# Two-layer hybrid encoder: the slots of four gates, of two placings, of one key head and of one low part

## The chip, the cores and the metric

The kernel runs on one core of a Trainium2 chip. The metric is the device time of one execution in microseconds (us). The engines are TensorE (PE: matrix products and transposes), VectorE (DVE), ScalarE (ACT), GpSimd (POOL) and SyncE (SP, here only a DMA queue). They run their own instruction streams and meet at semaphores.

## What is computed

Two layers (`DEPTH` 2) on 512 tokens of width 1024, float32. Each layer norms its input, projects it into 32 column heads of 128, runs four heads of differential attention and four heads of a gated linear recurrence in both directions, projects the eight head outputs back, and adds a convolutional gated feed-forward part of width 2816. Cut to what matters:

```
h = rms_norm(x, mix_norm_g[l])
proj = h @ w_in[l]
da_q, da_k, da_v, hg_q, hg_zf, hg_zb, hg_i, hg_g = split_cols(proj, IN_SIZES)
y_a = diff_attention(da_q, da_k, da_v, cos, sin, ...)   # q, k normed per half head, then rotated
y_b = hgrn2_bidirectional(hg_q, hg_zf, hg_zb, hg_i, hg_g, lower_bounds[l, 0], lower_bounds[l, 1], hg_out_g[l])
x = x + jnp.concatenate([y_a, y_b], axis=-1) @ w_out[l]
x = x + conv_glu_ffn(rms_norm(x, ffn_norm_g[l]), w_up[l], conv_w[l], conv_b[l], w_down[l])

def gates(z, lb):            # per head and direction
    log_f = log_sigmoid(z) + log1p(lb * exp(minimum(-z, 30)))
    key = (1 - lb) * sigmoid(-z)
```

In layer 0 the lower bounds are zero, so a gate there is only its sigmoids.

## The kernel before

**Products in parts.** Every weight and every large input is split into a high part (`wH`, `hH`, `yH`) and a low part (`wL`, `hL`, `yL`), and a product is three matmuls: high by high, low by high, high by low (lines 582 to 584). A *unit* is one weight tile of 128 by 1024. It is loaded into `raw` by SyncE, ScalarE copies its high part (`high_now`, line 914), and GpSimd subtracts to get the low part (`split`, line 512); in the eight slots `SPLITS` (7 to 14) VectorE does that (line 1431). A unit of the input projection is 24 matmuls over 512 tokens.

**Slots.** The mixer of a layer is written as 40 slots, `for s in range(SLOTS)`, on every engine. In slot s TensorE projects unit s in two halves, and the other engines do what hangs on the unit before it. The table `ORDER` says which head part unit s is: `dq`, `dk`, `dv` of attention, `hq`, `zf`, `zb`, `hi`, `hg` of the recurrence. Units 32 to 39 are the output projection. VectorE evicts unit s - 1 in slot s (`evict`, line 1348).

**What else a slot holds.** Each engine works through its stream in order, so the place of a call in the slot's body sets who waits for whom.

- Items 0 to 23 (`item_of`, from slot 7 on), twelve for each pair of recurrent heads. Items 0 to 7 are the levels of the intra-block scores: TensorE multiplies (line 672), VectorE grows the queries `QQ` by the forget products (line 1463), GpSimd grows the keys `KK` (line 545), ScalarE copies the keys crosswise to `kx` (line 1014). Levels 0 to 5 are gathered by masks in a small tile `quarters()`. Levels 6 and 7 stay in their banks 2 and 3. `assemble` on ScalarE places these three results in the score tile `A`: the gathered diagonal quarters (line 1026) and level 6 in the slot of item 6, level 7 in the slot of item 7 (line 1033). Items 8 and 9 (`TURN_F`, `TURN_B`) turn the keys to `KTOK` (line 686), item 10 (`CARRY`) multiplies them with the values (line 701) for VectorE's states `ST` (lines 1489 and 1491), and item 11 gathers everything.
- Steps 0 to 15 of attention (`step_of`, from slot 17 on), one query tile of one head each: scores (line 729), row maximum (line 1500), exponentials (line 1055), one slot later `combine` on VectorE (lines 1506 to 1511), the turn of `W` on TensorE (line 738), the copy `wT` on ScalarE (line 1047), and the values (line 747).
- Statistics (`STATS`: slot to head), the mean square of a head. ScalarE squares it (lines 971 and 972), VectorE forms the low part of the square (`square_low`, line 1383), TensorE multiplies by a mean matrix (`stat`, lines 632 and 633) at the end of the slot, and one slot later ScalarE makes the reciprocal root (`fin`, lines 948 and 951) and VectorE applies it: `rope` with rotary tables for `dk` and `dq` (lines 1360 to 1366), `norm` for outputs.
- `forget(i)`, four VectorE instructions (lines 1408 to 1411) that finish gate i in layer 1, by the table `FORGET`. In layer 0 VectorE instead prepares the rotary tables in the slots `ROTARY`, and the lower bounds in slot 16 (`bounds`).
- In slots 31 to 34 `FINISH` lists the output heads whose high part (`high_out`, ScalarE) and low part (`low_out`, VectorE, line 1397) are formed.

In slot 13 ScalarE also loads an activation table (line 938), and in layer 0 makes the sine and cosine (lines 1144 and 1145).

## Time and profile before

| | |
|---|---|
| median of 3 runs | 1372.3 us (1371.53 to 1372.79) |
| the profiled execution | 1371.9 us, of which the span of its instructions is 1370.1 |
| TensorE busy | 1341.0 us (98%) |
| VectorE busy | 914.3 us (67%) |
| ScalarE busy | 642.2 us (47%) |
| GpSimd busy | 661.0 us (48%) |
| TensorE busy from 0 to 345 us (layer 0, mixer) | 330.94 us |
| TensorE busy from 345 to 665 us (layer 0, feed-forward) | 320.00 us |
| TensorE busy from 665 to 1025 us (layer 1, mixer) | 348.03 us |
| TensorE busy from 1025 to 1370 us (layer 1, feed-forward) | 341.99 us |

Times of the trace count from the start of the span. A row of a timeline reads: start, duration, engine, line, operation, output from inputs, and how many; in brackets the engine's idle time ahead of it and whose result ended it. A duration of a row with "x4" covers the four. TensorE's matmuls overlap by some tenths of a microsecond, since a row runs to the modelled end of its results. Slot 13 of layer 0 begins at 88.0, slot 14 at 94.9; in layer 1 slot 13 begins at 768.5 and slot 14 at 775.3.

### The profile page before, as it was taken

The numbers are of one execution on the slowest core, as the hardware profiler recorded it, in microseconds if no ns is written. First come the engines' busy times: TensorE is split into PE (matmuls) and PEld (weight loads), VectorE is DVE, ScalarE is ACT, GpSimd is POOL, SyncE is SP. The second block draws the span as 40 slices with busy tenths as digits, with TensorE's granted clock in tenths as the row PEclk, the third lists the DMA queues.
The fourth block names the chain that finished last, engine by engine and source line by source line (L and its number), as shares of the span: only waits on it lengthen the run. The fifth ranks groups of instructions, "written<-read, shape, count | busy, mean of one in ns | idle before, by whom it ended". The sixth has DMA issues, their size and how long they took to land.

```text
span 1370.1 us, 20822 instructions
## 1 busy us (share of the span) xinstructions
PE 1341.0 (98%) x7970; PEld 1086.1 (79%) x7970; DVE 914.3 (67%) x1058; ACT 642.2 (47%) x948; POOL 661.0 (48%) x475
## 2 busy tenths in 40 slices
PE   9999999999999999999999999999999999999999
PEld 6777777877888888888877777778778888888887
DVE  7777898555888888600358789975658888885001
ACT  7453677574444444321443636666644444443121
POOL 2553565246444444444565536752474444444443
PEclk9999999999999999999999999999999999999999
DMA  5322122122332332333322222121233333333333
GB/s 186 94 78 85 51 71 74 46 63 92 100 100 92 96 105 92 93 106 96 92 93 94 78 70 71 55 70 46 78 92 94 105 94 93 102 98 92 95 104 108
DMA packets 37140, 121.43 MB, mean 89 GB/s; under 512 B 5056, under 2 KB 5440, under 8 KB 37056
## 3 DMA queue, kind: packets, MB, share of 16 engines
q1 hardware_dynamic: 36768, 119.75, 28.3%
q8 instruction: 58, 0.95, 0.3%
q10 hardware_dynamic: 288, 0.52, 0.1%
q14 instruction: 26, 0.21, 0.0%
HBM read 113.96 MB, written 2.10 MB: 85 GB/s over the span
## 4 chain that ended last, share of the span: by engine, by line
PE 77%; DVE 10%; ACT 5%; issue 4%; POOL 3%; DMA 0%; ACTq 0%; DVEq 0%; POOLq 0%
PE bank L582 23%; PE bank L584 23%; PE bank L583 23%; DVE QQ L1463 2%; PE bank L729 2%; POOL wL L518 1%; PE bank L747 1%; PE bank L672 1%; DVE hL L420 1%; POOL KK L545 1%; ACT wH L914 1%; POOL rstd L432 1%; PE bank L738 1%; PE bank L701 1%; ACT L938 1%
## 5 line engine op out<-in xcount | busy, mean ns | idle before, releaser
L518 POOL TENSOR_TENSOR wL<-raw,wH 128x1024 fp32r<-128x1024 f32 x142 | 344.2, 2424 | 403.3 <-ACT wH L914 293.1
L582 PE MATMUL bank<-hH,wH 128*128 128x512 f32 x1216 | 484.9, 399 | 2.1 <-DVE hL L420 2.0
L584 PE MATMUL bank<-hL,wH 128*128 128x512 f32 x1216 | 475.7, 391 | 0.0
L583 PE MATMUL bank<-hH,wL 128*128 128x512 f32 x1216 | 475.0, 391 | 0.0
L582 PEld LDWEIGHTS bank<-hH,wH 128*128 128x128 f32 x1216 | 229.2, 188 | 65.4 <-issue 14.5
L512 POOL TENSOR_TENSOR wL<-raw,wH 128x256 fp32r<-128x256 f32 x204 | 184.8, 935 | 197.4 <-ACT wH L914 197.4
L584 PEld LDWEIGHTS bank<-hL,wH 128*128 128x128 f32 x1216 | 229.0, 188 | 49.0
L583 PEld LDWEIGHTS bank<-hH,wL 128*128 128x128 f32 x1216 | 229.3, 189 | 45.4 <-issue 0.5
L914 ACT ACTIVATE wH<-raw 128x1024 fp32r<-128x1024 f32 x173 | 182.6, 1055 | 149.1 <-PE bank L584 149.0
L1617 DVE TENSOR_TENSOR x<-x,bank 128x512 f32<-128x512 f32 x16 | 10.9, 683 | 200.7 <-PE bank L584 200.7
L582 PE MATMUL bank<-gH,wH 128*128 (+1 forms) x352 | 137.3, 390 | 0.0
L584 PE MATMUL bank<-gL,wH 128*128 (+1 forms) x352 | 137.1, 389 | 0.0
L583 PE MATMUL bank<-gH,wL 128*128 (+1 forms) x352 | 137.1, 389 | 0.0
L1604 DVE TENSOR_TENSOR gL<-gt,gH 128x512 fp32r<-128x512 f32 x44 | 99.5, 2261 | 31.0 <-ACT gH L1187 31.0
L1591 DVE SCALAR_TENSOR_TENSOR ua<-uu,R,ua 128x511 f32<-128x511 f32 x44 | 107.2, 2436 | 1.5
L922 ACT ACTIVATE wH<-raw 128x1024 fp32r<-128x1024 f32 x36 | 38.1, 1059 | 146.4 <-PE bank L584 146.4
L1176 ACT ACTIVATE ua<-uu,R 128x512 f32<-128x512 f32 x44 | 35.9, 816 | 127.0 <-DVE uu L1582 127.0
L545 POOL TENSOR_TENSOR KK<-KK,T 128x512 f32<-128x512 f32 x56 | 79.6, 1441 | 27.3 <-PE bank L672 27.3
L1582 DVE TENSOR_TENSOR uu<-bank,rms 128x512 f32<-128x512 f32 x88 | 59.9, 685 | 44.6 <-PE bank L584 26.7
L582 PEld LDWEIGHTS bank<-gH,wH 128*128 128x128 f32 x352 | 66.1, 188 | 14.3 <-issue 0.7
L584 PEld LDWEIGHTS bank<-gL,wH 128*128 128x128 f32 x352 | 66.1, 188 | 13.7
L583 PEld LDWEIGHTS bank<-gH,wL 128*128 128x128 f32 x352 | 66.1, 188 | 13.7
(172 smaller groups left out, 1736.3 us busy)
## 6 DMA issues: line engine op xcount, KB each, us to landing
raw<-wts SPq DMA_DIRECT2D x210, 512.0 KB, 3.5
x<-xT SPq DMA_DIRECT2D x8, 256.0 KB, 5.8
swp<-K SPq DMA_DIRECT2D x32, 64.0 KB, 2.0
swp<-QO SPq DMA_DIRECT2D x32, 64.0 KB, 2.5
outT<-x SPq DMA_DIRECT2D x8, 256.0 KB, 2.0
raw<-wts ACTq DMA_DIRECT2D x2, 256.0 KB, 4.5
raw<-wts SPq DMA_DIRECT2D x2, 256.0 KB, 5.9
W<-pos SPq DMA_DIRECT2D x1, 256.0 KB, 5.3
```

The costliest lines, as they stand in the source:

```text
L512: m = pool.tensor_tensor(wL[:, s, at], raw[:, s, at], wH[:, s, at].bitcast(F32), ALU.subtract)
L518: pool.tensor_tensor(wL[:, s, :], raw[:, s, :], wH[:, s, :].bitcast(F32), ALU.subtract)\
L545: last = pool.tensor_tensor(v, v, w.to_broadcast([P, n, h]), ALU.mult)
L582: pe.matmul(out, wH[:, s, a:a + P], rhs_h, start=first, stop=False)
L583: pe.matmul(out, wL[:, s, a:a + P], rhs_h, start=False, stop=False)
L584: return pe.matmul(out, wH[:, s, a:a + P], rhs_l, start=False, stop=last)
L914: act.activation(wH[:, u % 2, :], raw[:, u % 2, :], ACT.Copy).then_inc(w_high.sem, 1)
L922: act.activation(wH[:, s, :], raw[:, s, :], ACT.Copy).then_inc(w_high.sem, 1)
L1176: act.activation(dst[:, q, :], uu[:, q, c, :], ACT.Identity, bias=conv(p, c, 3), scale=conv(p, c, 1))\
L1582: dve.tensor_tensor(uu[:, p % 2, c, :], bank[(2 * p + c) % 4][:], rms[:], ALU.mult).then_inc(up_ev.sem, 1)
L1591: dve.scalar_tensor_tensor(dst[:, q, 0:S - 1], uu[:, q, c, 1:S], conv(p, c, 2), dst[:, q, 0:S - 1], ALU.mult, ALU.add).then_inc(conv_done. ...
L1604: dve.tensor_tensor(gL[:, at], gt[:, p % 2, :], gH[:, at].bitcast(F32), ALU.subtract)\
```

## The change

Nothing is computed in another way. Five things change place:

1. `assemble` runs later. Level 6 is placed in the slot of item 7, level 7 in that of item 8, the gathered diagonal in that of item 9, each before that slot's own item; before, they stood behind the item, and a slot (the diagonal three slots) earlier. Since the diagonal's tile `quarters()` now lives longer than `KTOK` is free, it moves to the space of `ST`, and the states wait for the placing.
2. The turn of the forward keys waits for the first two placings only, and in the second pair, too, it comes behind the first half of the slot's unit.
3. The gates 4 to 7 of layer 1 are finished one by one at the ends of slots 10 to 13 instead of in pairs in slots 15 and 16.
4. The unit of the second key head (`("dk", 1)`) moves from index 17 to 15, `("hq", 2)` and `("hq", 3)` come one later, and its statistics move from slot 18 to 16 (so its `rope` from 19 to 17).
5. The low part of output head `("hgo", 0)` moves from slot 32 to slot 33, behind the last combination.

```diff
-         ("dk", 0), ("dq", 0), ("dv", 0), ("hq", 2), ("hq", 3),
-         ("dk", 1), ("dq", 1), ("dv", 1), ("dk", 2), ...
+         ("dk", 0), ("dq", 0), ("dv", 0), ("dk", 1), ("hq", 2), ("hq", 3),
+         ("dq", 1), ("dv", 1), ("dk", 2), ...
-STATS = {13: ("dk", 0), 14: ("dq", 0), 18: ("dk", 1), 19: ("dq", 1), ...
+STATS = {13: ("dk", 0), 14: ("dq", 0), 16: ("dk", 1), 19: ("dq", 1), ...
-FORGET = {3: (0,), 4: (1, 2), 5: (3,), 15: (4, 5), 16: (6, 7)}
+FORGET = {3: (0,), 4: (1, 2), 5: (3,)}
+FORGET_LATE = {10: 4, 11: 5, 12: 6, 13: 7}
+PLACE = {LEVELS - 1: LEVELS - 2, TURN_F: LEVELS - 1, TURN_B: None}
...
-            return KTOK[:, 0, 0, 0:2, :].rearrange("p n c -> p (n c)").rearrange("p (n t) -> p n t", t=QUARTER)
+            return ST[:, 0, 0, 0:2, :].rearrange("p n c -> p (n c)").rearrange("p (n t) -> p n t", t=QUARTER)
...
-                                pe.wait_ge(*a_set.at(l, 3 * pair + 3))
+                                pe.wait_ge(*a_set.at(l, 3 * pair + 2))
...
-                        if n is not None and n != TURN_F:
+                        if n is not None and n % PAIR_ITEMS != TURN_F:
                             item(n)
...
-                        if n == TURN_F:
+                        if n is not None and n % PAIR_ITEMS == TURN_F:
                             item(n)
...
                             if pair:
-                                act.wait_ge(*kv_mm.at(l, 4))
+                                act.wait_ge(*av_mm.at(l, 2))
...
-                        if lv == LEVELS - 2:
+                        if lv is None:
                             act.wait_ge(*a_msk.at(l, 5 * pair + 5))
-                            if pair:
-                                act.wait_ge(*av_mm.at(l, 2))
                             for g in range(4):
                                 rows = slice(g * QUARTER, (g + 1) * QUARTER)
                                 a = act.activation(spread(g, g, QUARTER), quarters()[rows], ACT.Copy)
                             a.then_inc(a_set.sem, 1)
+                            return
+                        if pair:
+                            act.wait_ge(*av_mm.at(l, 2))
...
                         if item_of(s) is not None:
+                            pair, lv = divmod(item_of(s), PAIR_ITEMS)
+                            if lv in PLACE:
+                                assemble(pair, PLACE[lv])
                             item(item_of(s))
-                            if item_of(s) % PAIR_ITEMS in (LEVELS - 2, LEVELS - 1):
-                                assemble(*divmod(item_of(s), PAIR_ITEMS))
...
                         if d == 0:
                             dve.wait_ge(*tot_ready.at(l, 7 * pair + 7))
+                            dve.wait_ge(*a_set.at(l, 3 * pair + 3))
...
                         if step_of(s - 1) is not None:
                             combine(step_of(s - 1))
+                        if s == N_IN + 1:
+                            low_out(FINISH[N_IN][1])
...
                         for p in FINISH.get(s, ()):
-                            if s != LATE or p < KT - 1:
+                            if p not in (FINISH[N_IN][1], KT - 1):
                                 low_out(p)
...
+                        if l and s in FORGET_LATE:
+                            forget(FORGET_LATE[s])
```

Below, instruction rows are given as line, operation, output from inputs and size. ScalarE in slots 13 to 15 of layer 0, before (`A` is the score tile, `rstd` and `sq` belong to statistics, `wH` is a unit's high part):

```order
L1014 ACTIVATE kx<-KK 128x1024
L1026 ACTIVATE A<-KTOK 32x8x32 x4
L1033 ACTIVATE A<-bank 32x8x32 x4
L1144 ACT_TABLE_LOAD
L1144 ACTIVATE cosT<-V 128x512
L1145 ACTIVATE sinT<-V 128x512
L938 ACT_TABLE_LOAD
L914 ACTIVATE wH<-raw 128x1024
L948 ACTIVATE rstd<-bank,C 128x512
L951 ACTIVATE rstd<-rstd 128x512
L971 ACTIVATE sqR<-QO 128x512
L972 ACTIVATE sq<-QO 128x512
```

The same place of the changed kernel, from the last row of slot 13's item on:

```order
L1148 ACT_TABLE_LOAD
L1148 ACTIVATE cosT<-V 128x512
L1149 ACTIVATE sinT<-V 128x512
L940 ACT_TABLE_LOAD
L916 ACTIVATE wH<-raw 128x1024
L950 ACTIVATE rstd<-bank,C 128x512
L953 ACTIVATE rstd<-rstd 128x512
L973 ACTIVATE sqR<-QO 128x512
L974 ACTIVATE sq<-QO 128x512
L1036 ACTIVATE A<-bank 32x8x32 x4
L916 ACTIVATE wH<-raw 128x1024
L950 ACTIVATE rstd<-bank,C 128x512
```

The two placings of slot 13 are gone; level 6 stands behind slot 14's squares, the diagonal in slot 16.

VectorE in slots 10 and 11 of layer 1, before (`ev` holds values to be turned, `QQ` the queries):

```order
L1431 TENSOR_TENSOR wL<-raw,wH 128x1024
L1463 TENSOR_TENSOR QQ<-QQ,T 128x128x4 x2
L1348 TENSOR_TENSOR ev<-bank,rms 128x512
L1442 COPY_PREDICATED KTOK<-M,bank 128x256
L1431 TENSOR_TENSOR wL<-raw,wH 128x1024
L1463 TENSOR_TENSOR QQ<-QQ,T 128x64x8 x2
```

And in the changed kernel:

```order
L1435 TENSOR_TENSOR wL<-raw,wH 128x1024
L1467 TENSOR_TENSOR QQ<-QQ,T 128x128x4 x2
L1412 SCALAR_TENSOR_TENSOR tmp<-T,KK 128x512
L1413 SCALAR_TENSOR_TENSOR T<-tmp,lball,T 128x512
L1414 TENSOR_SCALAR T<-T 128x512
L1415 TENSOR_SCALAR KK<-KK,omlb 128x512
L1352 TENSOR_TENSOR ev<-bank,rms 128x512
L1446 COPY_PREDICATED ST<-M,bank 128x256
L1435 TENSOR_TENSOR wL<-raw,wH 128x1024
L1467 TENSOR_TENSOR QQ<-QQ,T 128x64x8 x2
```

The four instructions of a gate stand between the growth of one level and the eviction of the next slot; slots 11 to 13 get the like.

VectorE in slots 32 and 33 of layer 0, before (`yL` is a low part, `W` the combination):

```order
L1397 TENSOR_TENSOR yL<-QO,yH 128x512
L1397 TENSOR_TENSOR yL<-QQ,yH 128x512
L1378 SCALAR_TENSOR_TENSOR QQ<-QQ,R,rstd 128x512
L1506 RECIPROCAL sm<-sm 128x2
L1507 TENSOR_TENSOR sm<-sm,lamc 128x1
L1508 TENSOR_SCALAR E<-E,sm 128x512
L1511 SCALAR_TENSOR_TENSOR W<-E,sm 128x512
L1390 TENSOR_TENSOR QQ<-QQ,T 128x512 x2
```

And in the changed kernel:

```order
L1401 TENSOR_TENSOR yL<-QO,yH 128x512
L1382 SCALAR_TENSOR_TENSOR QQ<-QQ,R,rstd 128x512
L1511 RECIPROCAL sm<-sm 128x2
L1512 TENSOR_TENSOR sm<-sm,lamc 128x1
L1513 TENSOR_SCALAR E<-E,sm 128x512
L1516 SCALAR_TENSOR_TENSOR W<-E,sm 128x512
L1401 TENSOR_TENSOR yL<-QQ,yH 128x512
L1394 TENSOR_TENSOR QQ<-QQ,T 128x512 x2
```

The low part of the recurrent head (`yL<-QQ,yH`) now stands behind `W`.

## Rows read from the trace of the kernel before

**Rows 1.** TensorE's waits: who waited for whom, us in total, times, longest.

```profile
PE bank L729 <- DVE QO L1366: 3.7, 2, 1.8
PE bank L632 <- DVE sqR L1383: 3.4, 2, 2.9
PE bank L738 <- DVE W L1511: 2.9, 3, 1.2
...
PE bank L729 <- ACT E L1055: 1.7, 1, 1.7
PE bank L632 <- ACT wT L1047: 1.7, 2, 0.8
...
PE bank L701 <- DVE ST L1491: 1.0, 1, 1.0
```

**Rows 2.** Timeline, ScalarE, layer 0: start, us, engine, line, operation, count, idle before.

```profile
93.37 1.67 ACT L1026 ACTIVATE A<-KTOK 32x256 f32<-32x256 f32 x4
95.06 1.53 ACT L1033 ACTIVATE A<-bank 32x256 f32<-32x256 f32 x4
...
100.38 1.06 ACT L914 ACTIVATE wH<-raw 128x1024 fp32r<-128x1024 f32 x1
...
103.76 1.18 ACT L1033 ACTIVATE A<-bank 64x512 f32<-64x512 f32 x2
104.96 1.06 ACT L914 ACTIVATE wH<-raw 128x1024 fp32r<-128x1024 f32 x1
...
106.76 0.72 ACT L951 ACTIVATE rstd<-rstd,C 128x512 f32<-128x512 f32 x1
```

**Rows 3.** Timeline, TensorE: statistics to turn of keys, layer 0, then layer 1.

```profile
104.63 0.80 PE L632 MATMUL bank<-sqR,meanR 128*128 128x512 f32 x1 [2.93 <-DVE sqR L1383]
...
109.32 0.81 PE L686 MATMUL bank<-C,KK 128*128 128x128 f32 x6
...
782.61 0.50 PE L632 MATMUL bank<-sqR,meanR 128*128 128x512 f32 x1 [0.48 <-DVE sqR L1383]
...
785.92 0.82 PE L686 MATMUL bank<-C,KK 128*128 128x128 f32 x6
```

**Rows 4.** Stretches: busy us by engine, granted clock, DMA share, GB/s.

```profile
105.00:107.00 2.00, 2.00 (x6) 1.52 (x6) 1.90 (x4) 1.94 (x3) 0.84 (x1) 0.50 0.24 96
846.00:848.00 2.00, 2.00 (x6) 1.59 (x5) 1.96 (x3) 1.06 (x1) 2.00 (x3) 0.50 0.28 72
```

**Rows 5.** Timeline, VectorE, layer 1: the last gate of the second pair.

```profile
800.56 1.22 DVE L1408 SCALAR_TENSOR_TENSOR tmp<-T,KK 128x512 f32<-128x512 f32 x1
801.82 0.75 DVE L1409 SCALAR_TENSOR_TENSOR T<-tmp,lball,T 128x512 f32<-128x512 f32 x1
...
803.06 0.48 DVE L1411 TENSOR_SCALAR KK<-KK,omlb 128x512 f32<-128x512 f32 x1
```

**Rows 6.** Timeline, GpSimd and VectorE: slot 10 of layer 0, then slot 13 of layer 1.

```profile
69.93 3.17 POOL L545 TENSOR_TENSOR KK<-KK,T 128x512 f32<-128x512 f32 x2
...
72.01 1.64 DVE L1307 SCALAR_TENSOR_TENSOR V<-V 128x512 f32<-128x512 f32 x1
...
768.57 0.69 DVE L1348 TENSOR_TENSOR K<-bank,rms 128x512 f32<-128x512 f32 x1 [1.44 <-PE bank L584]
```

**Rows 7.** Timeline, VectorE, layer 0: end of slot 19, start of slot 20.

```profile
149.07 0.69 DVE L1366 TENSOR_TENSOR K<-K,rstd 128x512 f32<-128x512 f32 x1
149.83 0.69 DVE L1348 TENSOR_TENSOR ev<-bank,rms 128x512 f32<-128x512 f32 x1
```

**Rows 8.** Timeline: values to be turned in slot 27 of both layers; low part, slot 32.

```profile
223.60 0.68 DVE L1348 TENSOR_TENSOR ev<-bank,rms 128x512 f32<-128x512 f32 x1
...
224.34 0.66 PE L617 MATMUL bank<-C,ev 128*128 128x128 f32 x4
...
282.20 0.69 DVE L1397 TENSOR_TENSOR yL<-QQ,yH 128x512 fp32r<-128x512 f32 x1 [1.09 <-ACT yH L1070]
...
903.76 0.68 DVE L1348 TENSOR_TENSOR ev<-bank,rms 128x512 f32<-128x512 f32 x1
```

More of the change, by code:

```diff
@@ L58 @@
 FIRST_ITEM, FIRST_STEP = 7, 17
-STATS = {13: ("dk", 0), 14: ("dq", 0), 18: ("dk", 1), 19: ("dq", 1), 20: ("hgo", 0), 21: ("dk", 2), 22: ("dq", 2),
+STATS = {13: ("dk", 0), 14: ("dq", 0), 16: ("dk", 1), 19: ("dq", 1), 20: ("hgo", 0), 21: ("dk", 2), 22: ("dq", 2),
          23: ("hgo", 1), 24: ("dao", 0), 25: ("dk", 3), 26: ("dq", 3), 27: ("dao", 1), 30: ("dao", 2),
```

2 rows, old and new, of the table ORDER are left out of this document.

## The prediction

> **What bounds the kernel now.** First the page's busy line, which stands in the table above: TensorE is busy nearly all of the span, so the change can only gain what TensorE stands still, plus what the clock costs it. Next the list of whom TensorE waited for [rows 1]: which producers hold it up, how often and for how long at most. Then the timelines around each of these waits, to see whose work lies in front of the producer. The two feed-forward parts and the output projection follow the mixer; there TensorE has almost no waits in the list, and their weight stream is paced by TensorE's own progress, so an idle microsecond removed from the mixer shortens the span by one.
>
> I call "slot s" the stretch in which TensorE projects unit s. Ten waits matter, and they come in pairs, one in each layer, or in one layer alone: the statistics product behind VectorE's low part of a square (2.9 us in layer 0, 0.5 in layer 1, together 3.4), the scores behind a rotated query (1.8 twice), the last turn behind the last combination (1.2 twice), the scores behind the exponentials (1.7, layer 1), the carry behind the states (1.0, layer 1), and the product behind the copy of wT (0.85 twice, 1.7 together) [rows 1].
>
> **Late placing, layer 0, slots 13 to 15.** ScalarE is the late one. It places the masked diagonal and level 6 in slot 13 (from 93.37 to 96.59, 3.22 us) in front of the table loads, the split of unit 15 and the squares whose low part TensorE waits for at 104.63 [rows 2, 3]. These 3.22 us leave that stretch: the high half of unit 15 starts at 97.16 instead of 100.38, the squares are done at about 100.6 instead of 103.8, and VectorE's low part, 0.7 us behind, is there at about 101.4. TensorE wants it at 104.63 - 2.93 = 101.7. The whole 2.93 us go. The half clock behind it goes too: between 105 and 107 the granted clock is 0.50, the 1.2 GHz level, right after this pause [rows 4]. The same instructions from the statistics product to the turn took 4.69 us here (104.63 to 109.32) and 3.31 in layer 1 at full clock (782.61 to 785.92), so it cost 1.4 us [rows 3].
>
> What comes late next is the turn of the forward keys in slot 15, which waits for both off-diagonal placings. Before, they lay a slot earlier. Now ScalarE does the squares (100.6), level 6 (1.53, to 102.2), the high half of unit 16 and the two steps of the query's root (2.52 us, 104.96 to 107.48), then level 7 (1.18): done at 105.9 [rows 2]. TensorE, started at 101.55, wants the turn 3.3 us later, at 104.9 [rows 3]. A new wait of 1.0. Net for layer 0: -2.93 - 1.4 + 1.0 = **-3.3 us**. Behind it, the diagonal (1.67) now lies in slot 16 ahead of the backward keys; there ScalarE waits for TensorE to finish its unit in any case, and the carry that needs the keys comes a unit later, so I cost it at nothing; without that cover it would be at most 1.7.
>
> **The same in layer 1.** Only 0.48 us stand there now [rows 3], and I let them go. In slot 15 ScalarE is not behind; it starts unit 16 when TensorE ends unit 14's slot: 2.52 + 1.18 = 3.7 against TensorE's 3.1 to 3.3, a new wait of 0.6.
>
> **Gates in slots 10 to 13, layer 1.** One gate is four VectorE instructions, 2.98 us from 800.56 to 803.54, and about 2.5 if the first, 1.22 there, takes no longer than the second, 0.75 [rows 5]. Four of them leave slots 15 and 16. They made VectorE so late that the fourth ended at 803.54; only then come the eviction of unit 16, the states and the row maximum, for which TensorE waits 1.0 and (by way of the exponentials) 1.7 [rows 1]: the carry and the scores of slot 18. In their place stand one low square and the rope of the second key, about 4 us against 12, so **-2.77 us**.
>
> Where they go, VectorE had some 1.4 us of idle ahead of each eviction (1.44 at 768.57) [rows 6], in slots of 6.8 us (768.5 to 775.3). A gate of 2.5 to 3.4 us makes VectorE up to 2 us late after each. What it owes TensorE there has room: the values to be turned are wanted only half a unit later, and the queries' growth ends 1.4 us before the unit does. I add up 0.3 at the statistics of slot 13 and 0.1 at slot 14. Bounds: 0 if the growth runs faster without GpSimd beside it, 3 if each slot's lateness adds (2.0 + 2 x 0.5). I take 0.4, since in layer 0 the same place in slot 10 holds a step of the rotary tables: GpSimd's pair ended at 73.10, and VectorE's instruction started at 72.01 and took 1.64 us against the 0.75 of its like [rows 5, 6]. The VectorE instruction paid, not GpSimd.
>
> A page of the Trainium skill speaks against this part: SBUF — State Buffer, section "SBUF: two separate sides", says that VectorE's instructions with two SBUF inputs and GpSimd's hold a common port pair as an exclusive lock for the whole instruction. By that rule a gate's first two instructions, if they come first, stop GpSimd's growth of the keys, on whose copy TensorE's next level waits; that result is the last rival. By that rule, the trace agrees for VectorE's side alone, in the row at 72.01.
>
> **The second key head two slots earlier.** The unit moves from index 17 to 15, its statistics from slot 18 to 16, its rope from slot 19 to 17; each of the two query units in between goes one later, still ahead of the preparation in slot 18. The four swap transfers go with it, ahead of the loads of units 19 and 20 on SyncE's queue; they wait for the eviction at the start of slot 16, and the load behind them waits for a split later in that slot, so the queue loses nothing. What the rope leaves in slot 19 gives TensorE nothing: there the rope ended at 149.76 and VectorE met the next unit at 149.83 [rows 7]. So the scores' wait of slot 21, 1.8 us in each layer behind the rope of the *query*, stays: **0**. In layer 0 slot 16 also has the gates' bounds, small instructions in a row; VectorE reaches slot 17 some 1 us late, and the scores and their exponentials have a whole unit's time there. Below zero is excluded only by this cover: without it, it is at most 1.
>
> **Slots 25 to 27.** ScalarE's 3.2 us of placing in slot 25 sit ahead of the copy of wT; they leave, and the 0.85 goes in each layer [rows 1]. But the turn of the forward keys in slot 27 (0.82, as at 785.92 [rows 3]) used to stand at the slot's start, while VectorE still worked on the values to be turned: they were ready at 224.28 and TensorE took them at 224.34 [rows 8], and the eviction ran without a pause in front of it. With that product half a unit later and VectorE bound by the scores of slot 26, TensorE stands still there for 0.75 in layer 0; in layer 1 they were ready at 904.44, some 0.4 ahead of TensorE, so it loses 0.35. Net **-0.1 and -0.5**.
>
> **Low part behind the last combination.** VectorE waited 1.09 us for ScalarE at 282.20 and did 0.69 us for head 0 before the combination [rows 8], which TensorE's turn waited 1.22 for [rows 1]. With it moved behind, the combination can start at 281.9 instead of 283.47; the turn's wait goes whole, and the low part is ready ahead of the second half of the unit. ScalarE's later work in slots 33 and 34 moves up with it: **-1.22** in each layer.
>
> **Sum.** Layer 0: -3.3 - 0.1 - 1.2 = -4.6. Layer 1: -0.5 + 0.6 + 0.4 - 2.8 - 0.5 - 1.2 = -4.0. Together -8.6 from the profiled execution's 1371.9 us, 1363.3; that execution lies 0.4 under the median of the three, so **1363.7 us**.
>
> **Rivals.** *The clock falls elsewhere.* A drop to 0.50 [rows 4] also followed the 1.8 us pause in layer 1's slot 21, but not the like pause in layer 0, nor 1.0 and 1.7 close together [rows 1]. Those two pauses of slot 21 stay, so none, one or two drops at 1.4 us each follow: 1362.3, 1363.7 or 1365.1. Nothing in the profile says which; it lies within my own range.
>
> *The gates make VectorE and GpSimd the bound in slots 11 to 14.* Beside GpSimd a gate may take 4.0 us (1.64 and 1.22 for the first two instructions, as in the rows, some 0.5 for the others and the gaps [rows 5, 6]); then the bound of 3 us stands in place of the 0.4, and the time is 1366.3. For it: VectorE's growth takes over 2 us beside GpSimd. Against: the rotary steps in layer 0.
>
> *ScalarE stays the bound of slots 13 to 16.* If its placings come late wherever they stand, slot 15 gives back 3 in layer 0 and 2 in layer 1 instead of 1.0 and 0.6: 1363.7 + 3.4 = 1367.1; with the last rival together 1369.7, no difference that can be measured.
>
> *Slower.* VectorE is busy 5.4 us of a slot's 6.8 (6.8 - 1.44) [rows 6]. With four gates at 4.0 it is 9.4, 2.6 late in each of four slots, 10.4; and if each gate also holds GpSimd by one 1.22 us instruction ahead of the key copy, 4.9 more: 1363.7 + 15.3 - 0.4 = 1378.6. It decides from 11.3 us of loss, 2.8 a slot. Against it is that in the timelines GpSimd's pair starts with VectorE's growth and ends before it, so that a gate behind the growth mostly finds GpSimd idle.
>
> **How the numbers follow.** The forecast with its clock cases 0.68, gates as bound 0.12, ScalarE as bound 0.08, both together 0.06, slower 0.03, unseen gains 0.03. A measurement of this kernel can tell about 0.2%, 2.7 us, from no change; so faster 0.90, same 0.07, slower 0.03. The range holds the forecast, its clock cases and the two middle rivals: 1360.8 to 1368.0.
>
> **What would show it.** Right: no wait at the statistics product of slot 14 in layer 0, granted clock 1.00 there; a wait of 0.6 to 1.0 at the turn of slot 15; no waits in layer 1 at the carry and the scores of slot 18; the scores of slot 21 still waiting 1.8; turns of slot 33 unwaited; a new wait at the turned values of slot 27. Wrong: TensorE waiting on VectorE's queries or GpSimd's keys over 1 us in layer 1's slots 11 to 14, or over 2 us at slot 15.

## The result and the profile after

| | before | after |
|---|---|---|
| median | 1372.5 us of 4 runs (1371.53 to 1372.79) | 1361.03 us of 4 runs (1360.56 to 1361.43) |
| profiled execution | 1371.9 us, span 1370.1 | 1361.43 us, span 1359.6 |
| TensorE busy | 1341.0 us | 1339.1 us |

The ratio after to before is 0.9922, with a 95% interval of 0.9910 to 0.9935: the change makes the kernel 0.8% faster. The forecast was 1363.7 us, and the median stands 2.7 under it, 0.2 above the lower end of the range (1360.8). The medians differ by 11.5 us and the two profiled executions by 10.5, where my sum had 8.6. Of the profiled ones, the one after lies 0.4 above its median and the one before 0.6 under; part of that is the clock, as the section on it shows.

The first view again is the list of whom TensorE waited for, in the kernel after (us in total, times, longest). It answers to [rows 1]; the line numbers are two to five higher than before.

```profile
PE bank L731 <- DVE QO L1370: 3.7, 2, 1.8
PE bank L674 <- DVE QQ L1467: 2.2, 2, 1.1
...
PE bank L619 <- DVE ev L1352: 1.8, 3, 0.6
...
PE bank L627 <- ACT sq L974: 1.5, 2, 0.8
...
PE bank L688 <- ACT A L1036: 1.4, 2, 0.9
PE bank L740 <- DVE W L1516: 0.4, 1, 0.4
```

The scores behind the rotated query still wait 1.8 us twice. The statistics product (3.4 before), the carry (1.0), the scores behind the exponentials (1.7) and the product behind wT (1.7) are gone from the list. The turn of `W` had 2.9 us in three waits: 1.2 at the last turn of each layer and 0.4 at that of slot 21 in layer 0. Only the 0.4 is left. New is the turn of the forward keys behind the placing of `A`: 0.9 and 0.5.

Layer 0, slots 14 and 15, ScalarE and TensorE, against [rows 2, 3]:

```profile
97.67 1.06 ACT L916 ACTIVATE wH<-raw 128x1024 fp32r<-128x1024 f32 x1
...
100.41 0.61 ACT L974 ACTIVATE sq<-QO 128x512 f32<-128x512 f32 x1
100.92 1.52 ACT L1036 ACTIVATE A<-bank 32x256 f32<-32x256 f32 x4
101.98 0.40 PE L634 MATMUL bank<-sqR,meanR 128*128 128x512 f32 x1
...
104.91 1.18 ACT L1036 ACTIVATE A<-bank 64x512 f32<-64x512 f32 x2
...
106.23 0.85 PE L688 MATMUL bank<-C,KK 128*128 128x128 f32 x6 [0.89 <-ACT A L1036]
```

The squares are done at 101.02, the statistics product at 101.98 has no idle time ahead of it, and the turn waits 0.89 us for level 7, which ends at 106.09. The clock stays at 1.00 in the stretch that had 0.50 in [rows 4] (columns as there):

```profile
105.00:107.00 2.00, 1.11 (x9) 0.80 (x8) 1.97 (x3) 1.29 (x4) 2.00 (x3) 1.00 0.01 4
```

Layer 1: the turn, then the products of slots 17 and 18 that had waited 1.0 and 1.7 us:

```profile
781.00 0.84 PE L688 MATMUL bank<-C,KK 128*128 128x128 f32 x6 [0.54 <-ACT A L1036]
...
799.77 1.28 PE L703 MATMUL bank<-HI,KTOK 128*128 128x128 f32 x10
800.98 1.13 PE L731 MATMUL bank<-K,QO 64*128 64x512 f32 x4
```

**Where the time went.** Take the same product in both traces, its start after less its start before: that tells how far TensorE is ahead at any point. Steps of that difference, by stretch:

| stretch | forecast | measured |
|---|---|---|
| start-up | 0 | +0.4 |
| layer 0, slots 13 to 15 | -3.3 | -3.5 |
| layer 0, slots 25 to 27 | -0.1 | -1.05 |
| layer 0, last combination | -1.2 | -1.2 (-1.36, then +0.17 in slot 34) |
| layer 1, slots 10 to 15 | +0.5 | +0.4 |
| layer 1, slots 16 to 18 | -2.8 | -3.4 |
| layer 1, slots 25 to 27 | -0.5 | -1.0 |
| layer 1, last combination | -1.2 | -1.2 |
| sum | -8.6 | -10.5 |

So by its stretches the forecast held, except in slots 25 to 27. Two of the rows are mostly scatter between executions. The code of the start-up is unchanged, and the same product early in the stream (line 591 before, at 22.71; 23.12 after) starts between 22.64 and 23.20 in the traces of this case. The changed kernel executed once more gains 0.3 us on the "after" trace in slots 10 to 13 of layer 1 (0.56 behind it at 742.41, 0.26 at 769.67). Whether each stretch moved for the reason given is another question, and for one of them it did not.

### The profile page after: what moved, and what is told of

Read it like the earlier page. It is cut to its first block, busy times and chain, and to the rows that moved or that the text cites. A ratio compares the mean times of both kernels' runs of the same rounds, so it can differ in the third digit from the quotient of the medians.

```text
span 1359.6 us, 20826 instructions
## 1 busy us (share of the span) xinstructions
PE 1339.1 (98%) x7970; PEld 1084.7 (80%) x7970; DVE 911.3 (67%) x1058; ACT 641.9 (47%) x948; POOL 659.5 (49%) x475
## 4 chain that ended last, share of the span: by engine, by line
PE 80%; DVE 9%; ACT 4%; issue 4%; POOL 2%; DMA 0%; ACTq 0%; DVEq 0%; POOLq 0%
PE bank L584 24%; PE bank L586 24%; PE bank L585 24%; PE bank L731 2%; DVE QQ L1467 2%; POOL wL L520 1%; PE bank L674 1%; PE bank L749 1%; DVE hL L422 1%; ACT wH L916 1%; PE bank L703 1%; PE bank L740 1%; POOL rstd L434 1%; DVE sqR L1387 1%; PE bank L619 1%
## 5 line engine op out<-in xcount | busy, mean ns | idle before, releaser
L1600 DVE SCALAR_TENSOR_TENSOR ua<-uu,R,ua 128x511 f32<-128x511 f32 x44 | 111.3, 2529 | 1.5
```

Of the source, the lines that this page charges most:

```text
L1600: dve.scalar_tensor_tensor(dst[:, q, 0:S - 1], uu[:, q, c, 1:S], conv(p, c, 2), dst[:, q, 0:S - 1], ALU.mult, ALU.add).then_inc(conv_done. ...
```

## The experiments

All times are medians of 4 or 5 runs; each variant starts from the changed kernel (1361.03), and names what it undoes. Where the granted clock of a whole execution matters it is given: it is 1.000 where the trace shows no fall to the 1.2 GHz level, and 0.999 with one short fall.

### Each part undone by itself

**Late placing undone.** Placings, their space, their waits and the turn's place are as before; the part of it that moves the calls:

```diff
-                            pair, lv = divmod(item_of(s), PAIR_ITEMS)
-                            if lv in PLACE:
-                                assemble(pair, PLACE[lv])
                             item(item_of(s))
+                            if item_of(s) % PAIR_ITEMS in (LEVELS - 2, LEVELS - 1):
+                                assemble(*divmod(item_of(s), PAIR_ITEMS))
```

> The changed kernel with the late placing undone (and what belongs to it: the tile of the gathered quarters back in KTOK, the turn of the second pair back at the start of slot 27); gates, second key head and low part stay as changed. Ledger of the prediction: 3.3 us in layer 0, 0.1 and 0.5 in slots 25 to 27, minus 0.1 in layer 1's slots 14 and 15 come back, 3.8 in all: 1361.0 + 3.8 = 1364.8. Rival, the ledger that the two traces give (a wait that goes takes some 0.16 us more with it than its idle time, and slots 25 to 27 gave 1.0 in each layer): 3.5 + 2.0 = 5.5, 1366.5. By either, the clock falls again in slot 14 of layer 0.

Measured: 1366.02 us (1364.53 to 1368.12), 5.0 more. Its trace has the old waits back:

```profile
104.76 0.80 PE L634 MATMUL bank<-sqR,meanR 128*128 128x512 f32 x1 [2.93 <-DVE sqR L1385]
...
213.44 0.47 PE L634 MATMUL bank<-sqR,meanR 128*128 128x512 f32 x1 [0.87 <-ACT wT L1049]
...
783.89 0.49 PE L634 MATMUL bank<-sqR,meanR 128*128 128x512 f32 x1 [0.57 <-DVE sqR L1385]
```

and 0.85 us at slot 25 of layer 1. The table's steps give 3.5 + 1.05 in layer 0 and 1.0 in layer 1, 5.5 in all: the ledger made from both traces (1366.5) was nearer than the one of the prediction (1364.8). Slots 25 to 27 are worth 1.0 in each layer.

How much comes back depends on the clock behind the 2.93 us pause. The profiled execution is the slowest of the five: its clock is low there for longer than before (a granted clock of 0.50 over 107 to 109 us, where the kernel before has 0.86), and from the statistics product to the turn it takes 6.05 us (104.76 to 110.81) against the 4.69 of [rows 3]. In two of the five the granted clock was 1.000, so it fell behind no pause at all; they took 1364.53 and 1364.72, which is 4.0 above the 1360.56 of the changed kernel's execution at 1.000. So the 1.4 us of the clock belongs to some executions only.

**Gates back in slots 15 and 16.**

```diff
-FORGET = {3: (0,), 4: (1, 2), 5: (3,)}
-FORGET_LATE = {10: 4, 11: 5, 12: 6, 13: 7}
+FORGET = {3: (0,), 4: (1, 2), 5: (3,), 15: (4, 5), 16: (6, 7)}
+FORGET_LATE = {}
```

> The changed kernel with the four late gates of layer 1 back in slots 15 and 16 in pairs. Ledger of the prediction: 2.8 - 0.4 = 2.4 us come back, 1363.4. Ledger of the traces: 3.4 - 0.2 = 3.2, 1364.2. Rival, that this part and the second key head's move hang together: the second key's low square and rope now stand behind the gates in slots 16 and 17, VectorE is later by another 0.7 at the states and by 3 at those of slot 18, and the gather waits as well: 1365.5 to 1368.

Measured: 1367.48 us (1366.58 to 1367.67), 6.5 more: the rival with the linked parts was right. The second key's statistics stand in slot 16 now, and VectorE reaches their low square only behind four gates. Timeline, then the stretch (busy PE, PEld, DVE, ACT, POOL; granted clock; DMA share; GB/s):

```profile
793.98 1.22 DVE L1387 TENSOR_TENSOR sqR<-sq,sqR 128x512 fp32r<-128x512 f32 x1
795.25 0.80 PE L634 MATMUL bank<-sqR,meanR 128*128 128x512 f32 x1 [4.80 <-DVE sqR L1387]
```

```profile
795.00:800.00 5.00, 4.75 (x18) 3.80 (x18) 2.64 (x8) 1.32 (x2) 2.15 (x3) 0.50 0.36 96
```

That is one wait of 4.80 us, and the 1.2 GHz level for all of the 5 us shown. The 6.5 us hold both.

**Second key head back at index 17 and slot 18.**

```diff
-         ("dk", 0), ("dq", 0), ("dv", 0), ("dk", 1), ("hq", 2), ("hq", 3),
+         ("dk", 0), ("dq", 0), ("dv", 0), ("hq", 2), ("hq", 3), ("dk", 1),
...
-STATS = {13: ("dk", 0), 14: ("dq", 0), 16: ("dk", 1), ...
+STATS = {13: ("dk", 0), 14: ("dq", 0), 18: ("dk", 1), ...
```

> The changed kernel with the unit of the second key head back at index 17 and its statistics in slot 18. The prediction costed this part at nothing: 1361.0 within 0.3, the scores of slot 21 still waiting 1.8 in both layers. Rival, that the earlier key makes VectorE's slots 19 and 20 shorter and so helps the rotated query: 1362 or more, a wait over 1.8 in slot 21.

Measured: 1360.97 us (1360.53 to 1361.41). The part is worth nothing, as costed, and the scores of slot 21 wait 1.82 us in both layers here, 1.83 with the early key.

**Low part back ahead of the last combination.**

```diff
-                        if s == N_IN + 1:
-                            low_out(FINISH[N_IN][1])
...
-                            if p not in (FINISH[N_IN][1], KT - 1):
+                            if s != LATE or p < KT - 1:
```

> The changed kernel with the low part of the recurrent head 0 back in slot 32. The prediction: 1.2 in each layer comes back, 1361.0 + 2.4 = 1363.4, with a wait of 1.2 at the last turn. Rival, that the gain was given back by ScalarE's table loads in slots 33 and 34 (the wait at the statistics of slot 34 grew from 0.59 to 0.76 us): 1362 or less.

Measured: 1362.70 us (1362.53 to 1363.60), 1.7 more. Four of these five executions had a granted clock of 1.000; against the changed kernel's execution at 1.000 the fastest is 2.0 more, and by the two traces, with one fall each, it is 2.2. TensorE, layer 0:

```profile
282.96 0.63 PE L740 MATMUL bank<-C,W 128*128 128x128 f32 x4 [1.21 <-DVE W L1516]
...
290.55 1.13 PE L627 MATMUL bank<-sq,C 128*128 128x512 f32 x2 [0.57 <-ACT sq L974]
```

The changed kernel has no wait at that turn, and 0.76 in place of 0.57 at the last statistics: a sixth of the gain is given back one slot later.

**Late gates left out.** This kernel leaves the work out instead of moving it, so its layer 1 does not compute the reference's result; it is built only to price the gates. In `forget`:

```diff
+                        if i >= 4:
+                            dve.tensor_scalar(k[:, 0:1], k[:, 0:1], omlb[:, n:n + 1], None, ALU.mult).then_inc(z_done.sem, 1)
+                            return
```

> The changed kernel in which gates 4 to 7 of both pairs' second half are not finished in layer 1: of the four instructions of each only the last is left, on one column, so layer 1's forget factors and keys of the second pair are not the reference's. It measures what the gates cost in slots 10 to 13. The prediction: they are hidden but for some 0.4 us, 1360.6. Ledger of the traces: 0.04 + 0.17 + 0.05, 1360.8. Rival, the lock on the common port (a gate's first two instructions hold GpSimd's growth of the keys, on whose copy TensorE's next level waits): up to 3 us, 1358, and GpSimd's pairs of slots 11 to 14 shorter by 0.7 each without the gates.

Measured: 1361.04 us (1360.16 to 1361.15), the same as with the gates. Four gates in slots 10 to 13 cost nothing that a median shows. By the two traces they make the second statistics product of slot 14 in layer 1 0.27 us later, and 0.15 of that is won back at the turn of slot 15, which waits 0.54 with them and 0.66 without. Their rows in the kernel after, slot 10 and the first gate row of slot 11, layer 1:

```profile
745.19 3.17 POOL L547 TENSOR_TENSOR KK<-KK,T 128x512 f32<-128x512 f32 x2
747.26 1.64 DVE L1412 SCALAR_TENSOR_TENSOR tmp<-T,KK 128x512 f32<-128x512 f32 x1
748.94 0.75 DVE L1413 SCALAR_TENSOR_TENSOR T<-tmp,lball,T 128x512 f32<-128x512 f32 x1
...
755.26 0.68 DVE L1412 SCALAR_TENSOR_TENSOR tmp<-T,KK 128x512 f32<-128x512 f32 x1
```

GpSimd's pair ends at 748.36. The gate's first instruction, issued into it, takes 1.64 us; the same one in slot 11, with no GpSimd work beside it, 0.68. So it is VectorE that pays, about 1.0 us there, as the rotary step did in [rows 6]. The Trainium skill, SBUF — State Buffer, section "SBUF: two separate sides", says that of a VectorE instruction with two SBUF inputs and a GpSimd one that reads SBUF, whichever starts first holds the shared port pair for its whole length and the other blocks. By that rule, the trace agrees: GpSimd had started first, and VectorE's instruction ends at 748.90, 0.54 us behind the end of the pair. The slower rival needed a gate's first two instructions to start ahead of a pair of GpSimd's and run into it. In slots 11 to 13 they end before it starts, and the pairs of slots 11 to 14 are no longer with the gates (3.15, 3.11, 3.06 and 3.04 us) than without (3.60, 3.10, 3.06 and 2.95).

### Why did the waits of slots 17 and 18 go?

My forecast put the 2.8 us there down to the gates. One kernel puts both the gates and the second key back (the two diffs above together), so that nothing stands behind the gates that did not before.

> The changed kernel with two parts undone together: the gates 4 to 7 of layer 1 stand in slots 15 and 16 again, and the unit and statistics of the second key head at index 17 and slot 18. Theory 'linked parts' (the late gates cost what the trace of the kernel before showed, 1.03 at the carry and 1.74 at the scores of slot 18 plus some 0.2 for each pause, less the 0.4 of the gates in slots 10 to 13; the 6.5 us lost with the gates alone undone came from the second key's statistics, which then stood behind them): 1361.0 + 3.2 - 0.4 = 1363.8, between 1363.3 and 1364.5, with pauses of 1.0 and 1.7 at the carry and the scores of slot 18 of layer 1 and no pause at its statistics in slot 16. Theory 'gates alone' (the 6.5 us hang on the gates wherever the key stands): 1367.5, with the pause somewhere in slots 16 to 18 of about 4.8 us. Theory 'the clock did it' (most of the 6.5 was a lower clock, not the pause): the same pauses as in the first theory, but a granted clock of 0.5 behind them, 1365 to 1366.

Measured: 1361.16 us (1360.76 to 1361.73), as none of the three theories has it. With the gates where they were in the kernel before, the carry does not wait, and the scores of slot 18 wait a third:

```profile
798.35 1.50 PE L703 MATMUL bank<-HI,KTOK 128*128 128x128 f32 x12
...
800.42 1.13 PE L731 MATMUL bank<-K,QO 64*128 64x512 f32 x4 [0.57 <-ACT E L1058]
```

The other cause stands three slots earlier, in VectorE's low part of unit 15, for which it has to wait for ScalarE. First the kernel before, ScalarE and then VectorE, and below it this run:

```profile
773.80 1.68 ACT L1026 ACTIVATE A<-KTOK 32x256 f32<-32x256 f32 x4
775.51 1.53 ACT L1033 ACTIVATE A<-bank 32x256 f32<-32x256 f32 x4
...
778.35 1.06 ACT L914 ACTIVATE wH<-raw 128x1024 fp32r<-128x1024 f32 x1
...
779.44 1.23 DVE L1431 TENSOR_TENSOR wL<-raw,wH 128x1024 fp32r<-128x1024 f32 x1 [3.81 <-ACT wH L914]
```

```profile
770.54 1.23 DVE L1435 TENSOR_TENSOR wL<-raw,wH 128x1024 fp32r<-128x1024 f32 x1 [0.67 <-ACT wH L916]
```

VectorE stood 3.81 us behind the high part that ScalarE copied only after the two placings of slot 13. In this run TensorE is 5.8 us ahead at that point, so of the 8.9 us between the two rows of VectorE 3.1 are its own. From there on VectorE has no idle time in either trace until it evicts the unit in front of the carry, at 803.47 before and 795.07 here, 8.4 us apart: 2.6 of the 3.1 us of lateness had run through growth, rope and gates to slot 17. It was visible in the trace of before, and I had read only the wait nearest to TensorE.

**Late placing undone, and the second key back**: against the kernel before, only the late gates and the late low part are left. This asks whether the early gates would have done it by themselves.

> The late placing and the second key head's move undone; against the kernel before it keeps only the late gates and the late low part. After the last run (gates and key undone, 1361.16, with the pause at the carry of layer 1 gone all the same and 0.57 us in place of 1.74 at the scores of slot 18) the theory is 'two remedies for one wait': VectorE's lateness in slots 15 to 17 of layer 1 came from ScalarE's placings in slot 13, behind which VectorE stood 3.81 us at 779.44, and either taking these placings away or taking the gates away cures it. Then the gates alone, with the placings back, still remove the pauses at the carry and the scores of slot 18: the time is that of the run without late placing, 1366.0 within 0.7. Theory 'the gates cure nothing by themselves': the pauses of 1.0 and 1.7 stand there again and the time is that of the kernel before less the low part's 1.7, 1370.4.

Measured: 1365.65 us (1364.24 to 1367.39), with no wait at the carry or at the scores of slot 18:

```profile
804.50 1.50 PE L703 MATMUL bank<-HI,KTOK 128*128 128x128 f32 x12
805.92 1.13 PE L731 MATMUL bank<-K,QO 64*128 64x512 f32 x4
```

That is 6.5 us below the kernel before (1372.11 in the same session) by the medians, 4.8 by the profiled executions (1367.12 against 1371.9), and 5.8 at a granted clock of 1.000 (1364.24 and 1364.56 against 1369.80 to 1370.52 in five executions of the kernel before). The low part's 2.0 to 2.4 and the 3.4 of the two waits, less at most 0.4 for the gates, make 5.0 to 5.8. So the waits took two causes together, ScalarE's placings in slot 13 and the gates in slots 15 and 16, and they had two remedies: placing late leaves 0.57 of their 2.77 us, gates early leaves nothing. The change makes both, and in this version the second brings nothing that a median shows (1361.16 without it).

### The lower clock behind the pause of slot 21

Of the two pauses of 1.8 us in slot 21, the granted clock fell only behind that of layer 1 in the traces before and after; in other variants it fell in layer 0, in both or in none. The changed kernel once more, unaltered:

> The changed kernel once more, unaltered. If the lower clock behind the 1.8 us pause of slot 21 belongs to the code and its timing, the trace shows it again in layer 1 (835 to 840 us) and not in layer 0, and the time is 1361.0 within 0.5. If it belongs to the execution, it stands elsewhere (in layer 0, in both or in none), and the time goes with it: 1359.5 with none, 1361.0 with one, 1362.5 with two.

Measured: 1361.03 us (1360.78 to 1361.68). First the execution shown as "after", then this one:

```profile
160.00:165.00 5.00, 4.25 (x18) 2.67 (x19) 4.90 (x8) 2.22 (x3) 5.00 (x5) 1.00 0.22 54
835.00:840.00 5.00, 4.91 (x14) 3.03 (x15) 4.89 (x8) 2.21 (x3) 5.00 (x5) 0.66 0.21 52
```

```profile
160.00:165.00 5.00, 4.86 (x14) 3.30 (x15) 4.90 (x8) 2.21 (x3) 5.00 (x5) 0.66 0.22 54
835.00:840.00 5.00, 4.19 (x17) 2.60 (x18) 4.89 (x7) 2.22 (x3) 5.00 (x5) 1.00 0.21 52
```

The same code had its fall in the other layer. So the place belongs to the execution, not to the change. Its price can be read in this one trace, from the scores of slot 21 to a product three slots on, layer 0 (with the fall) and layer 1 (without):

```profile
160.14 1.13 PE L731 MATMUL bank<-K,QO 64*128 64x512 f32 x4 [1.83 <-DVE QO L1370]
...
192.01 0.66 PE L619 MATMUL bank<-C,ev 128*128 128x128 f32 x4 [0.66 <-DVE ev L1352]
...
835.38 1.13 PE L731 MATMUL bank<-K,QO 64*128 64x512 f32 x4 [1.84 <-DVE QO L1370]
...
839.91 0.63 PE L740 MATMUL bank<-C,W 128*128 128x128 f32 x4 [0.43 <-DVE W L1516]
...
856.24 0.66 PE L619 MATMUL bank<-C,ev 128*128 128x128 f32 x4 [0.55 <-DVE ev L1352]
...
866.59 0.66 PE L619 MATMUL bank<-C,ev 128*128 128x128 f32 x4 [0.65 <-DVE ev L1352]
```

The stretch takes 31.87 us with the fall (160.14 to 192.01) and 31.21 without (835.38 to 866.59): a fall costs 0.7 here, not the 1.4 of slot 15. It takes 1.4 at first as well: the turn of slot 21 starts 5.49 us behind the scores with the fall (at 165.63) and 4.53 without, of which 0.43 is a wait. But the slower TensorE does not meet the waits of 0.43 and 0.55 that the other layer has.

Whether it falls at all differs too. Seven runs here pause 1.8 us in slot 21 of both layers and nowhere longer; in eleven of their 32 executions the granted clock was 1.000. The changed kernel took 1360.56 and 1360.78 in its two such executions, and 1360.92 to 1361.68 in the other six. The kernel before took 1369.80 to 1370.52 in five executions at 1.000 of 36, and had a median near 1372. So without any fall the change is worth some 9.6 us, and the rest of the 11.5 between the medians goes with the clock.

### A faster version

The list after names what is left: 1.8 us twice behind the rope of the second query, 0.9 and 0.5 behind level 7. Two edits, alone and together. **Rope ahead of the growth in slot 20**, on VectorE (its call at the old place in that slot is dropped):

```diff
+                        if s == 20:
+                            rope(ROPES.index(STATS[19]))
                         if n is not None:
                             grow(pair, lv)
```

> The changed kernel with the rope of the second query ahead of the growth of level 1 in slot 20 instead of behind it. If the 1.83 us at the scores of slot 21 come from the growth in front of the rope, they go, and TensorE waits some 0.4 for the grown queries at level 2 instead: -1.4 - 0.16 in each layer, 1361.0 - 3.0 = 1358.0, or 1356.4 if the clock does not fall in layer 1. Rival, that the wait only changes its name (level 2's queries, or GpSimd's keys behind the products of the forget factors): 1361.0.

Measured: 1358.89 us (1358.80 to 1359.16), 2.1 less and not 3.0 or 4.6. The growth that now comes second is late instead, and the combination of slot 22 too:

```profile
158.21 0.77 PE L674 MATMUL bank<-QQ,kx 128*32 128x32 f32 x64 [0.54 <-DVE QQ L1467]
...
173.12 0.63 PE L740 MATMUL bank<-C,W 128*128 128x128 f32 x4 [0.70 <-DVE W L1516]
```

In each layer 1.83 us go, with the 0.42 at the turn of slot 21 where it stood (layer 0), and 0.54 + 0.70 come. The step of TensorE's stream is 0.8 in layer 0 and 1.4 in layer 1, where 0.7 is the fall of the clock that this trace does not have.

**Level 7 placed ahead of the root in slot 15**, on ScalarE (again without its call at the old place):

```diff
+                        if item_of(s) == TURN_F:
+                            assemble(0, PLACE[TURN_F])
                         if s - 1 in STATS and s - 1 != LATE:
                             fin(STATS[s - 1])
```

> The changed kernel with level 7 of the first pair placed ahead of the two root steps in slot 15. If the wait of 0.89 and 0.54 at the turn of slot 15 is ScalarE's order, both go with 0.16 each: 1361.0 - 1.7 = 1359.3. Rival, that the root, 1.2 us later, makes the first query's rope and the scores of slot 17 late, or that ScalarE is late in any order: 1361.0.

Measured: 1359.44 us (1359.33 to 1360.11), 1.6 less, with no wait at the turns.

**Both:**

> Both of the last two edits. They lie in different slots, so their gains add: 1361.0 - 4.7 = 1356.3 (1354.7 if the clock does not fall in layer 1). Rival, that one of them shifts the other's work into a new wait: less than the sum by over 0.5.

Measured: 1356.92 us (1356.86 to 1356.97), ratio to before 0.9891 (0.9876 to 0.9906); 4.1 less than the change, where 4.7 was expected. It is the 2.1 and the 1.6, and 0.4 more. The granted clock is 1.000 in all four executions, as in the four with the rope moved alone, so the rest may be the clock; against the changed kernel's fastest execution, at 1.000 too, it is 3.7 less.

**Both, with gates and second key back where the kernel before had them:** are these two parts idle in the faster kernel too?

> The version with both improvements (rope of the second query ahead of the growth in slot 20, level 7 placed ahead of the root in slot 15; 1356.92), with the gates back in slots 15 and 16 of layer 1 and the second key head back at index 17 and slot 18. Theory 'two remedies': with the placing late these two parts of the change bring nothing; 0.4 saved in slots 10 to 13 against 0.57 at the scores of slot 18, so 1357.1, between 1356.6 and 1357.7. Theory 'both are needed once the other pauses are gone' (level 7 ahead of the root takes ScalarE's and so VectorE's margin in slot 15): the pauses at the carry and the scores of slot 18 grow, 1358.5 to 1360.

Measured: 1359.54 us (1358.69 to 1360.54), 2.6 more, or 1.8 to 2.0 by the two executions at a granted clock of 1.000 (1358.69 and 1358.89). The theory of two remedies falls short here:

```profile
799.43 1.79 PE L731 MATMUL bank<-K,QO 64*128 64x512 f32 x4 [1.74 <-ACT E L1058]
```

The wait is back in its old size, and the granted clock falls to 0.68 between 800 and 805. In slot 16 TensorE is 2.4 us ahead of the run with gates and key back (ScalarE's `wH`, which waits for it, at 782.00 against 784.41), but VectorE, busy without a pause behind its gates, comes to the eviction in front of the carry only 1.0 ahead (794.08 against 795.07). VectorE's lead is 1.4 us short of TensorE's, enough for the growth of the wait, 1.74 - 0.57 = 1.17. Taking TensorE's wait of slot 15 away spent the margin that had covered this one. Which of the two parts brings the 2.6, gates or key, no run separates here.

## Why the prediction came out, and which steps did not

**Right, by its own steps.** Slots 13 to 15 of layer 0: the squares done at 101.0 (forecast 100.6), statistics unwaited, the clock up, a new wait of 0.89 (1.0) in the turn; together -3.5 for -3.3. The turn of layer 1: 0.54 for 0.6. The second key: 0, undone by itself. The gates where they went: VectorE and not GpSimd pays, and the cost is hidden. The 0.4 put down for them is 0.1 by the traces with and without them; that slots 10 to 15 as a whole moved by +0.4 for +0.5 is partly scatter, since the second execution of the same code moved by 0.2 there. The scores of slot 21 stay at 1.83.

**Right number, wrong cause.** The -2.8 for the carry and the scores of slot 18 stood under the gates. The runs give it to either part: placing late takes the carry's wait and 1.2 of the scores' 1.7 with the gates where they were, gates early take both with the placings where they were. The step that failed is "They made VectorE so late that the fourth ended at 803.54": the four gates were in the queue, but without the 3.1 us that VectorE had lost three slots earlier they cost only 0.57. "Only 0.48 us stand there now, and I let them go" is the other half: with the gates in slots 15 and 16 the late placing is worth nearly as much in layer 1 as in layer 0, through VectorE instead of TensorE. In the run that keeps it without gates and key, TensorE's lead over the kernel before grows from 5.7 to 8.4 us in slots 16 to 18; a forecast for the late placing alone would have missed these 2.7.

**A link not seen.** I costed the second key at 0 and the gates at -2.8 as if they could be had apart. With the early key the gates have to be out of slots 15 and 16: 6.5 us hang on them there, and 0.1 with the key back.

**Mis-sized: slots 25 to 27.** Forecast -0.1 and -0.5, measured -1.05 and -1.0. The wait of 0.85 gave 1.1 when it went, in each layer. And I put a new wait of 0.75 and 0.35 at the turned values of slot 27. In layer 0 it isn't there:

```profile
218.19 0.69 DVE L1370 TENSOR_TENSOR K<-K,rstd 128x512 f32<-128x512 f32 x1
218.26 3.48 POOL L514 TENSOR_TENSOR wL<-raw,wH 128x256 fp32r<-128x256 f32 x4 [1.39 <-ACT wH L916]
218.80 0.68 DVE L1352 TENSOR_TENSOR ev<-bank,rms 128x512 f32<-128x512 f32 x1
...
219.54 0.66 PE L619 MATMUL bank<-C,ev 128*128 128x128 f32 x4
```

The kernel before, at the same place:

```profile
222.41 1.27 DVE L1366 TENSOR_TENSOR K<-K,rstd 128x512 f32<-128x512 f32 x1
222.41 3.26 POOL L512 TENSOR_TENSOR wL<-raw,wH 128x256 fp32r<-128x256 f32 x4 [1.31 <-ACT wH L914]
```

The last instruction of the rope started together with GpSimd's split then and took 1.27 us; now it starts 0.07 ahead of it and takes 0.69. I had held VectorE's durations fixed. That the 0.58 us is what closes the gap is read from the two traces; no run moved the split alone. And the order of start does not explain it by itself. In layer 1 of the kernel before, the same pair of instructions started 0.01 us apart, GpSimd's first, and VectorE's took 0.69:

```profile
903.14 3.56 POOL L512 TENSOR_TENSOR wL<-raw,wH 128x256 fp32r<-128x256 f32 x4 [1.31 <-ACT wH L914]
903.15 0.69 DVE L1366 TENSOR_TENSOR K<-K,rstd 128x512 f32<-128x512 f32 x1
```

So in layer 1 this instruction had nothing to gain, and some of the new wait is left: the scores of slot 27 start 10.11 us ahead of the kernel before, the turned values behind them 9.95 (904.91 to 894.96), so 0.16 of the 0.35 is lost. I had counted the moved product at its row's 0.82 us, but it moved the scores by 0.66.

**Mis-sized: each wait.** Waits that left whole gave more than their listed idle time: at the last turn 1.22 are listed and the stream moved by 1.36; in slots 16 to 18 it is 2.77 and 3.4. Part of it is that the rows behind a pause are longer: that of the carry has 1.90 us at 805.17 behind its pause and 1.50 at 798.35 without one.

**Mis-sized: a fall of the clock.** Priced at 1.4 wherever it comes; in slot 21 it costs 0.7. Between the two profiled executions this did not matter, with one fall there before and one after. The fall of slot 14 was taken as certain, and its 1.4 us as a gain; two of five executions without the late placing and five of 36 of the kernel before do without it.

**The range.** The median lies below even the clock case of 1362.3, and inside the range by 0.2 us: what was missing in slots 25 to 27, the 0.6 beyond the listed waits of slots 16 to 18 and the clock of the executions all went the same way. That the range held is partly luck.

**The rivals.** Gates as the bound and the slower case are refuted by the run without gates (no difference in the medians). ScalarE as the bound of slots 13 to 16 is refuted by the turns' waits of 0.89 and 0.54.

## What to carry to other kernels

A wait in front of the busiest engine names the last link only: follow the producer back through its stream to where it last stood idle, and ask who held it there, before the wait is booked to whatever is queued just ahead. When a change has several parts, undoing one alone can mislead. Here the gates alone undone cost 6.5 us, the key alone undone 0, and both together 0.1, since the late placing had cured the wait already; in a faster version the same two cost 2.6. So undo parts in pairs as well, before one is dropped or praised, and again when margins have shrunk.

## What the runs showed of the hardware

The same code in two executions had its clock at the 1.2 GHz level behind a 1.83 us pause once in layer 0 and once in layer 1, so a single trace doesn't tell which of two like pauses is followed by a fall; and with the 2.93 us pause of slot 14 in place, two of five executions without the late placing had no fall at all (granted clock 1.000, 1364.53 and 1364.72 us). The price of a fall depends on the waits behind it: 1.4 us in slot 15 before, where none followed soon, and 0.7 in slot 21, where two short ones (0.43 and 0.55) vanished. Beside GpSimd a VectorE instruction with two SBUF inputs took 1.64 us where it started 1.10 us before the end of a running pair, against 0.68 alone. Where it and GpSimd's split started within 0.1 us of each other it took 0.69 us (0.07 ahead), 1.27 (together) and 0.69 (0.01 behind); what decides there stays open.
